# Mixture-of-experts block: experts ordered by load with 32, 64 or 96 slots, down weights fetched on ScalarE's queue

## The reference, cut to what matters

```
logits = rmsnorm(x) @ w_router + b_router          # 288 x 32
gates, experts = softmax(top_4(logits))            # 288*4 = 1152 assignments
for each assignment (token t, expert e, gate g):
    h = xn[t] @ w_gate_up[e] + b_gate_up[e]         # 1024 -> 2048
    h = min(h_even, 7) * sigmoid(1.702*min(h_even, 7)) * (clip(h_odd, -7, 7) + 1)
    x[t] += g * (h @ w_down[e] + b_down[e])         # 1024 -> 1024
```

## Time and profile before

| what | value |
|---|---|
| median of the three runs | 1284.44 us |
| the profiled execution: time, span of the core | 1288.95 us, 1287.2 us |
| TensorE matmul busy | 1197.6 us (93%) |
| VectorE, ScalarE busy | 433.1 us (34%), 213.9 us (17%) |
| moved by DMA | 462.53 MB, mean 359 GB/s |
| MATMUL instructions on gu_ring | 2240, of dn_ring 1120 |

### The profile page before, as it was taken

The page is one execution under the profiler, slowest core; times in us unless marked ns, Lnnn a source line. Parts: engine busy times, 40 slices in busy tenths (PEclk is TensorE's granted clock), DMA queues, the critical chain, the costliest instruction groups (busy, mean ns, idle before and its releaser), DMA issues.

```text
span 1287.2 us, 15615 instructions
## 1 busy us (share of the span) xinstructions
PE 1197.6 (93%) x5780; PEld 506.2 (39%) x5780; DVE 433.1 (34%) x878; ACT 213.9 (17%) x423; POOL 2.7 (0%) x6
## 2 busy tenths in 40 slices
PE   7878888999999999999999999999999999999997
PEld 5657765333333333333333333333333333333332
DVE  6887423233333322332222222232223322223232
ACT  3394222111111111111111111111111111111111
POOL 0000000000000000000000000000000000000000
PEclk9967898899999999999999999999999999999999
DMA  8411067799999999999999999999999999989990
GB/s 334 133 37 71 1 267 325 301 416 420 417 422 420 420 422 421 422 420 421 421 417 420 422 421 420 422 420 422 420 418 422 421 420 421 419 351 364 401 407 39
DMA packets 67526, 462.53 MB, mean 359 GB/s; under 512 B 8724, under 2 KB 10388, under 8 KB 12848
## 3 DMA queue, kind: packets, MB, share of 16 engines
q1 hardware_dynamic: 65728, 459.98, 87.0%
q10 hardware_dynamic: 1728, 2.11, 0.5%
q0 software_dynamic: 48, 0.15, 0.0%
HBM read 457.61 MB, written 2.51 MB: 357 GB/s over the span
## 4 chain that ended last, share of the span: by engine, by line
PE 87%; DVE 8%; ACT 2%; issue 1%; ACTq 1%; DVEq 0%
PE banks L434 82%; DVE xT L1539 2%; DVE raw L1515 2%; PE banks L722 2%; PE banks L745 2%; ACT gath L1044 2%; PE banks L765 1%; DVE G_rot L1281 0%; DVE Tz L339 0%; ACTq L847 0%; DVE c L1273 0%; DVE c L1287 0%; ACTq L842 0%; DVE c L1288 0%; DVE c L1274 0%
## 5 line engine op out<-in xcount | busy, mean ns | idle before, releaser
L434 PE MATMUL banks<-gu_ring,xe 128*64 128x512 f32 x2240 | 506.2, 600 | 0.9 <-ACT xe L1049 0.7
L1539 DVE TENSOR_TENSOR xT<-xT,banks 128x576 f32<-128x576 f32 x144 | 102.3, 751 | 569.5 <-PE banks L434 569.5
L434 PEld LDWEIGHTS banks<-gu_ring,xe 128*64 128x64 f32 x2240 | 156.1, 138 | 303.9 <-issue 299.2
L434 PE MATMUL banks<-dn_ring,hT 128*64 128x512 f32 x1120 | 248.0, 595 | 0.0
L434 PEld LDWEIGHTS banks<-dn_ring,hT 128*64 128x64 f32 x1120 | 77.3, 137 | 145.8 <-issue 145.8
L434 PE MATMUL banks<-gT,ye 64*128 64x288 f32 x560 | 93.1, 441 | 15.5 <-DVE xT L1539 13.0
L434 PE MATMUL banks<-x_tok,oh 96*64 96x512 f32 x432 | 101.9, 607 | 1.2 <-DVE oh L1501 1.2
L1059 ACT ACTIVATE raw<-banks 128x512 f32<-128x512 f32 x35 | 20.9, 597 | 447.2 <-PE banks L434 447.2
L1515 DVE COPY raw<-banks 128x512 f32<-128x512 f32 x35 | 24.2, 692 | 179.3 <-PE banks L434 179.3
L434 PEld LDWEIGHTS banks<-gT,ye 64*128 64x128 f32 x560 | 45.4, 185 | 73.2 <-DVE xT L1539 41.6
L1068 ACT ACTIVATE ye<-banks 128x512 f32<-128x512 f32 x35 | 20.9, 597 | 225.1 <-PE banks L434 225.1
(11 more groups left out here) (293 smaller groups left out, 728.0 us busy)
## 6 DMA issues: line engine op xcount, KB each, us to landing
gu_ring<-w_gu_dram SPq DMA_DIRECT2D x280, 1024.0 KB, 10.0
dn_ring<-w_dn_dram SPq DMA_DIRECT2D x140, 1024.0 KB, 7.3
w_out<-w_out_dram SPq DMA_DIRECT2D x2, 2048.0 KB, 7.8
w_in<-w_in_dram SPq DMA_DIRECT2D x3, 1024.0 KB, 16.1
w_in<-w_in_dram SPq DMA_DIRECT2D x4, 512.0 KB, 10.0
W<-W1c SPq DMA_DIRECT2D x16, 128.0 KB, 2.3
w_glu<-w_glu_dram SPq DMA_DIRECT2D x1, 2048.0 KB, 8.7
xT<-xT_dram SPq DMA_DIRECT2D x2, 576.0 KB, 5.9
```

The lines of the kernel that those rows point to most:

```text
L434: return nc.tensor.matmul(out, lhsT, rhs, start=start, stop=stop, **kw)
L1539: X.tensor_tensor(two, two, pair[(1, 3)[c % 2]].rearrange("p (h f) -> p h f", h=2)[:, :, 0:T], ALU.add).then_inc(S("acc_done"), 1)
```

## The change

The experts run in an order that VectorE computes from the counts (`key`, `rank`, `ord_e`, semaphore `order_ready`), and each of the 32 positions has a kind that is fixed when the kernel is built. `mid` is the 64-slot pass as before. `few` has 32 slots. `many` has both: places 0 to 63 go through the 64-slot code, places 64 to 95 through the 32-slot code. Expert 0 stays at position 0; the four with the highest counts among the others get `many`, the nine with the lowest get `few`. Each engine reads the expert of a position from `ord_e` with a register load. Items are still possible, from 64 + `extra` tokens on (`extra` is 32, 0 or -32).

```diff
+FEW = 32
+BODY, ROUNDS = ("few", "many", "few", "mid"), 4
+KINDS = ["mid"] + list(BODY) * ROUNDS + ["few"] + ["mid"] * 14
...
     def load_first(sp):
         for k in range(8):
-            load_gu(sp, 0, k)
-        for j in range(2):
-            for c in range(4):
-                load_dn(sp, j, c, j)
+            sp.dma_start(gu_ring[k][:], a["w_gu"][0, k]).then_inc(gu_in[k], 16)
+        for c in range(4):
+            sp.dma_start(dn_ring[c][:], a["w_dn"][0, c]).then_inc(dn_in[c], 16)
...
     def load_others(sp):
+        sp.wait_ge(S("order_ready"), 1)
         with sp.Fori(0, PAIRS - 1) as i:
-            for k in range(8):
-                gu(i * 2 + 1, i * 2, k)
-            for c in range(4):
-                sp.wait_ge(S("dn_used"), i * 8 + (c + 1))
-                load_dn(sp, i * 2 + 2, c, 0)
...
+            x = [expert_at(k, i * 2 + (k + 1)) for k in range(2)]
+            gu(x[0], i * 2)
+            gu(x[1], i * 2 + 1)
...
+        def gather_s(g):
+            pe.wait_ge(S("oh_s_ready"), g + 1)
+            for t in range(3):
+                for q in range(4):
+                    last = mm(pb[7][FEW * q:FEW * q + FEW, 0:2 * P], oh_s[0:MT, t], x_tok[t][0:MT, q * 2 * P:(q + 1) * 2 * P],
+                              t == 0, t == 2, tile_position=(0, FEW * q))
...
     (gate_up, for each chunk k)
+                if kind != "few":
+                    for part in range(2):
+                        for h in range(2):
+                            f = part * D + h * HALF
+                            last = mm(pb[part][SLOTS * h:SLOTS * h + SLOTS, :], xe[:, k % 4, k // 4],
+                                      gu_ring[k][:, f:f + HALF], k == 0, k == KT - 1, tile_position=(0, SLOTS * h))
...
+                if kind != "mid":
+                    for q in range(4):
+                        last = mm(pb[5][FEW * q:FEW * q + FEW, :], xe_s[:, k % 2, k // 2],
+                                  gu_ring[k][:, q * HALF:(q + 1) * HALF], k == 0, k == KT - 1, tile_position=(0, FEW * q))
...
     (down, for each chunk c, after the 64-slot matmuls if there are any)
+                if kind != "mid":
+                    if c == 0:
+                        pe.wait_ge(S("h_s_ready"), s + 1)
+                    for kk in range(2):
+                        f = 2 * c + kk
+                        for q in range(4):
+                            last = mm(pb[7][FEW * q:FEW * q + FEW, 0:2 * P], hT_s[:, f % 4, f // 4],
+                                      dn_ring[4 * j + c][:, kk, q * 2 * P:(q + 1) * 2 * P], f == 0, f == KT - 1,
+                                      tile_position=(0, FEW * q))
...
     (combine, for each c and h)
+                    dst = pb[(2, 6)[c % 2] + h][:, 0:T]
+                    if kind != "few":
+                        rows = slice(SLOTS * h, SLOTS * h + SLOTS)
+                        last = mm(dst, ye[rows, c * P:(c + 1) * P], gT[rows], True, kind == "mid")
+                    if kind != "mid":
+                        q = 2 * h + c // 2
+                        rows = slice(FEW * q, FEW * q + FEW)
+                        last = mm(dst, ye_s[rows, (c % 2) * P:(c % 2 + 1) * P], gT_s[rows], kind == "few", True,
+                                  tile_position=(FEW * q, 0))
...
     (end of expert on TensorE)
+            if after != "few":
+                gather(w_after)
+            if after != "mid":
+                gather_s(s_after)
+            if after != "few":
+                turn_gathered(w_after)
+            if after != "mid":
+                turn_gathered_s(s_after)
+            if kind != "mid" and after != "mid":
+                pe.wait_ge(S("copied_s"), s_after * 2 + 2)
+            down(w, s, kind, j, fill)
...
     (ScalarE)
+        def next_down(p, j):
+            act.reg_load(reg_dn, ...)
+            x = act.snap(reg_dn, min_val=0, max_val=NE - 1)
+            for c in range(4):
+                load_dn(act, x, c, j)
...
+        def act_expert(p, w, s, kind, before, after, fetch):
...
+            if kind != "few":
+                act_tanh(w)
+            if after != "few":
+                act_gathered(w_after)
+            if after != "mid":
+                act_gathered_s(s_after)
+            if kind == "many":
+                act_tanh_s(s)
+            if after != "few":
+                act_turned(w_after)
+            if after != "mid":
+                act_turned_s(s_after)
+            if kind == "few":
+                act_tanh_s(s)
+            if kind != "few":
+                act_result(p)
+            if kind != "mid":
+                act_result_s(p)
+            if fetch is not None:
+                next_down(p + 2, fetch)
...
     (VectorE, once, after the gates)
+        ids = iota[:, 0:NE]
+        link(X.scalar_tensor_tensor(out=key[:], in0=cnt[:], scalar=float(SLOTS), in1=ids, op0=ALU.mult, op1=ALU.subtract))
+        link(X.memset(key[:, 0:1], float(SLOTS * P * P)))
+        link(X.tensor_tensor(ahead[:], wide(key[:], 1, NE), wide(key[:], 2, NE), ALU.is_gt))
+        link(X.tensor_reduce(rank[:], ahead[:], AX.X, ALU.add))
+        link(X.tensor_tensor(ahead[:], wide(rank[:], 1, NE), wide(rank_at, 2, NE), ALU.is_equal))
+        link(X.tensor_tensor(ahead[:], ahead[:], wide(ids, 1, NE), ALU.mult))
+        link(X.tensor_reduce(term, ahead[:], AX.X, ALU.add))
+        X.tensor_copy(ord_e[:], term).then_inc(S("order_ready"), 1)
```

More of the change, by code:

```diff
@@ L43 @@
 PAIRS = NE // 2
+FEW = 32
+BODY, ROUNDS = ("few", "many", "few", "mid"), 4
+KINDS = ["mid"] + list(BODY) * ROUNDS + ["few"] + ["mid"] * 14
+WIDE = [sum(k != "few" for k in KINDS[:p]) for p in range(NE + 1)]
+SLIM = [sum(k != "mid" for k in KINDS[:p]) for p in range(NE + 1)]
+N_WIDE, N_SLIM = WIDE[NE], SLIM[NE]
+N_MANY = KINDS.count("many")
+N_FEW = KINDS.count("few")
 EPS = 1e-6
@@ L729, in gate_up @@
             for k in chunks:
[L730 to L737, removed]
+                pe.wait_ge(gu_in[k], p * 16 + (16 + W_IN[k]))
@@ L801, in expert @@
                 gate_bias()
             else:
-                combine(e)
-            gate_up(e, e, range(5, 8))
-            pe.wait_ge(S("acc_done"), e * 4 + 4)
-            turn_hidden(e)
-            gather(e + 1)
-            turn_gathered(e + 1)
-            down(e, j, fill)
+                combine(p, w_before, s_before, before)
+            gate_up(p, w, s, kind, range(5, 8))
+            pe.wait_ge(S("acc_done"), p * 4 + 4)
+            if kind != "few":
+                turn_hidden(w)
@@ L821, in _ @@
+        for p in (17, 18):
+            expert(p, WIDE[p], SLIM[p], KINDS[p], KINDS[p - 1], KINDS[p + 1], p % 2, p // 2 + 1)
+        with pe.Fori(0, 6) as i:
+            for k in range(2):
+                expert(i * 2 + (19 + k), i * 2 + WIDE[19 + k], N_SLIM, "mid", "mid", "mid", (19 + k) % 2,
+                       i + ((19 + k) // 2 + 1))
+        expert(NE - 1, N_WIDE - 1, N_SLIM, "mid", "mid", "mid", 1, PAIRS)
+        turn_gates(N_WIDE)
+        combine(NE, N_WIDE - 1, N_SLIM, "mid")
         pe.wait_ge(S("list_ready"), 1)
@@ new lines, in expert @@
+        def expert(p, w, s, kind, before, after, x):
+            x_before, x_now, x_after = x
+            w_after, s_after = w + (kind != "few"), s + (kind != "mid")
+            if before != "bias":
+                if before != "few":
+                    gated(slots_of(x_before), bass.ds(x_before, 1), w)
+                if before != "mid":
+                    gated_s(slots_of(x_before), SLOTS if before == "many" else 0, bass.ds(x_before, 1))
+            if after != "few":
+                build_oh(slots_of(x_after), w_after)
+            if after != "mid":
+                build_oh_s(slots_of(x_after), SLOTS if after == "many" else 0, None if isinstance(p, int) and p == 0 else s_after)
+            accumulate(p)
+            if kind != "few":
+                hidden(p, w, s, x_now)
+            if kind != "mid":
+                hidden_s(s, w + s + (kind != "few"), x_now)
```

402 lines of the change are left out of this document (270 added, 132 removed).

## The result

| | time, us (lowest to highest) | ratio to before, 95% |
|---|---|---|
| before | 1284.3 | 1 |
| after | 1250.7 (1246.9 to 1252.8) | 0.974, 0.970 to 0.979 |
| predicted | 1210.5 (1184 to 1250) | |

What follows compares the result with a forecast made beforehand. TensorE and DMA (about 422 GB/s) were both taken as full. Profiled 1288.95 - 91.8 (items) + 18.8 (rounds) - 8.0 (position 17) + 8 (position 18) - 1 (first pass) = 1215.0, 1210.5 at the median; range 1184 to 1250.

Steps and rivals of the forecast that it cites:

- The step that failed: Combine of a many, run in the pass behind it: 8 us against 3.1, unknown by -9 to +8 in all.
- my 27.2: Length in us of a few pass behind a many, with two gate transposes (+0.4) and that combine (+4.9).
- rounds: Four rounds of few, many, few, mid: 124.5 us each against 119.8, +18.8 in all.
- items: Three items for experts with counts above 64 disappear from the end: -91.8 us.
- position 18: TensorE waits for gate/up data there because two short passes ahead have used up the slack: +8 us.
- Rival B: Clock falls to half in the waits of each of nine few passes: +31 us, 1241; chance 0.24.
- rival C: Packing falls short in narrow matmuls, four tiles bringing 3.1 instead of 4: +46 us, 1257; chance 0.10.
- D: Narrow steps take twice the time, only two tiles at work: 1356 us, slower than before; chance 0.03.
- `many` at 45.1: Length in us of a many pass: chunks 23.0, gates and combine 3.8, transposes and copies 6.6, down 11.7.
- The queue at 0: Moving down-weight DMAs to ScalarE: its 2.5 us is covered and a second issuing queue gains nothing, 0 us.
- `mid` in a round: A 64-slot pass in a round loses 1.3 us to the narrower gather, gains 0.5 of waits: 29.2.
- Rival A: Data bound: shape changes free and waits covered, DMA sets the pace, 1185 us; chance 0.13.

Runs made afterwards that it cites:

- e1: After, with the two 64-row combine matmuls of a step issued next to each other, then the two 32-row ones; 1225.9 us (0.958).
- e7: e1 and e2 together on after: combine grouped by shape, down weights on SyncE's queue chunk by chunk; 1203.0 us (0.937).
- e2: After, with the down weights back on SyncE's queue, chunk by chunk as each buffer is used; 1247.3 us (0.973).
- e5: e1 and e4 together on after, down weights still requested by ScalarE; 1215.0 us (0.947).
- e12: After, with the many combine ordered wide lower, narrow upper, wide upper, narrow lower rows; as many shape changes; 1251.4 us (0.977).
- e3: After, with 64-slot passes instead of 32-slot ones behind the four many passes; 1277.6 us (0.995).
- e8: The kernel before, with only the down weights of experts 2 to 31 requested by ScalarE after its results; 1283.1 us (0.999).
- e9: e5 with the four down chunks requested on SyncE's queue, all together once the last was used; 1192.1 us (0.929).
- e10: e1, e4 and e2 together on after, plus e3's 64-slot passes behind many; 1219.7 us (0.947).
- e11: e1, e4 and e2 together on after, plus wide gate/up matmuls ahead of narrow ones per chunk group in many; 1189.8 us (0.925).
- e4: After, with TensorE's copied_s wait in many moved from ahead of the 64-slot down matmuls to the first 32-slot one; 1252.6 us (0.977).

## Why the prediction was wrong

**The step that failed** is in the part on `many`: "Its combine alternates 64-row and 32-row matmuls into one bank, so little of it can overlap ... 32 of them and 16 changes of shape are 10.1; with a quarter of the time overlapped and the changes free, 5.8. I take 8, the middle, against 3.1." It measured 15.45. At full clock it would be 16 x 0.68 = 10.9, none of it overlapped, a little over the upper end of 10.1 (a MATMUL of 288 columns took 0.26 us in the first pass, where I had 0.24): 2.9 more than my 8. Then the clock falls and the second half takes 1.25 a pair, 4.6 more, and the chunks behind take 1.8 more. That is 2.9 + 4.6 + 1.8 = 9.3 of the 9.5 us by which each such `few` is longer than my 27.2; four of them make the +37.9 of the table. So two things were wrong in this one term: half of its range rested on an overlap for which I had no row (2.9 us), and the whole of it on full clock (6.4 us). The second is the larger.

**e1** bears this out as far as it goes: grouped by shape, the combine takes 5.5 us at full clock, and these four passes are 46.7 us shorter. It also shows that the term isn't the whole story. By the prediction's sum, a combine of 5.5 instead of 8 would give 1210.5 - 10 = 1200.5; e1 took 1225.9. Most of the difference is the second queue: without it, e7 took 1203.0.

**The other terms nearly cancel, by luck.** Measured less predicted, on the profiled execution: rounds +47.5, position 17 +0.8, items +0.4, position 18 -3.7, and the part ahead of position 1 -7.2, which I don't credit to the change. Together +37.8, from 1215.0 to 1252.8. That this is so close to the +37.9 of the four passes is chance: the +3.0 of `many` and the +6.1 of `mid` are offset by a short first pass.

**Rival B** was right about the event and nearly about its size, and wrong about the place. I tied the fall of the clock to the 4 us of waits in each `few`, and priced 3.4 us in nine passes, 31 in all, with a chance of 0.24. Passes of one kind at different clocks let its cost be estimated: 6.4 in each of the four combines and the chunks behind, 1.5 more in two of these passes (37.45 against 35.9), 3.3, 3.3 and 1.4 in three `many` (against 43.85), 1.6 in two `few` behind a `mid` (23.9 against 22.3), 1.3 at position 17 (22.7 against 21.4 in e2). That is some 41 us. It does come with waits (behind 583.54 in `many`, over position 17 of e5), but most of it fell in a combine in which TensorE never waited. The earlier trace rows had shown just that, a combine on 32 rows and then half clock; I read it for `few` and not for the long combine of `many`.

**Why the clock falls there stays open in part.** e1 shows that the grouped order of the same MATMULs keeps it. But the first pass's combine has no change of shape, and the clock fell behind it in after and e1 (0.50 at 232 to 234), though not in e12 (1.00 over 230 to 240) or e3. What it shares with the alternating combine is MATMULs one behind another on a part of the rows. No run separates that from the changes of shape.

**Right as they stood.** The items: the last combine's second half of after,

```profile
1243.67 1.42 PE L459 MATMUL banks<-gT,ye 64*128 64x288 f32 x8 [0.37 <-DVE xT L1765]
```

ends the kernel without a pass of 64 behind position 31 (against 1280.26 in the earlier trace rows), and 23 x 64 = 1472 wide and 13 x 64 = 832 narrow MATMULs on `gu_ring` are what the page counts. Fourfold packing: 598.80 to 601.52 is 24 x 0.107 + 0.15, so rival C falls, and D with it. The change of shape in the chunks: a wide and a narrow group start 1.87 and 1.00 us apart, 2.87 against my 2.88. `many` at 45.1 lies within 43.9 to 47.1, if for reasons that partly cancel: its real time without the fall of the clock is 43.9.

**Position 18.** I had +8 and it measured +4.3, for the reason given: two short passes had used up the slack. But the mechanism was larger than I saw. I wrote that the four chunks share the engines and leave 9 us of slack instead of 19, and let it act only there. It acts wherever TensorE catches up with the data, and the slower combine had hidden it.

**The queue at 0** is right for after (e2: 3 us, within the intervals) and for before (e8). It is not right for the change without its flaw: 23 us (e5 against e9, 1215.0 to 1192.1). The term that the prediction put at nothing is the second step that failed; the first one hid it. The Trainium skill's page "DMA: Bandwidth & Descriptors", section "Issuing engines are not separate DMA queues", says that a second issuing engine saves only issue time. The rate agrees, 420 to 422 GB/s with either. What e5 and e9 add is that a second queue changes the order of landing: what is needed late gets half the engines ahead of what is needed now.

**`mid` in a round** was 31.2 in three of four, not 29.2. The 2 us are one row, at the turn from one round to the next:

```profile
527.16 2.44 PE L459 MATMUL banks<-gu_ring,xe_s 128*32 128x512 f32 x16 [1.96 <-issue]
```

"issue" means that the profile shows nothing waited for. The fourth round, which doesn't turn back, lacks it (29.19), and so do the rounds of e3 and e10, which end on the same kind of pass behind another `mid` (29.1). Why only these have it stays open; no run was made for it.

**Rival A**, bound by data at 1185, is close to where the change arrives once both flaws are mended: 1189.8 in e11.

## What to carry to other kernels

When matmuls of two tile shapes alternate, count the changes and take the price with no overlap: each one cost 0.15 to 0.2 us here, and the 11 us stretch of nothing but such changes lost the clock as well, in every pass that had it. Order them by shape, which here was two lines for 25 us. Give a second DMA queue only transfers that are as urgent as those of the first, and before you move one, ask which queue TensorE will wait on once it is faster; that answer can't be had from a kernel in which something else is late.

## What the runs showed that I had not expected

- The granted clock fell to 0.50 while TensorE was busy 2.00 of each 2 us, about 5.5 us after the alternating combine began: in after, e12 and e3 alike. It stayed at full in e1's combine of the same 32 MATMULs (581.10 to 586.58) and in the chunks behind. A profile that shows TensorE busy all the time doesn't promise full clock.
- MATMULs of two shapes with disjoint rows and different banks don't overlap (0.68 us a pair in e12), those of one shape on disjoint rows do (0.68 us for four in e1).
- Two DMA queues with work in both shared the engines about evenly: waited-for chunks came 4.96 us apart in after, e4 and e5, where one takes 2.48.
- Gains don't add when a buffer stands between them: e1 alone is worth 25 us, one queue alone 3, both together 48.
